# Choice of experts on 128 candidate cells with 16-bit matches, roots taken from sums of squares, and weightings between the two remainders of a slab in V

## The chip, the cores and the metric

The kernel runs on one core of a Trainium2 chip. The metric is the device time of one execution in microseconds (us), lower is better; of several runs the median is taken. The engines are TensorE (PE in the profile's rows), VectorE (DVE), ScalarE (ACT), GpSimd (POOL) and the queues that issue DMAs (SP for SyncE's). Each runs its own list of instructions in order and waits on semaphores for the others.

## The reference

Two small transformer stacks, one behind the other, on 256 tokens of width 1024. The first has gated linear attention, then sliding-window attention, each followed by a PEER layer; the second has an mLSTM mixer, an MLA mixer and two MLPs. Everything is in float32. What the change touches is the choice in PEER, and the norms:

```python
def rmsnorm(x, g):
    y = x * lax.rsqrt(jnp.mean(x * x, axis=-1, keepdims=True) + EPS)

def block(xb):                                   # 128 tokens
    q = (xb @ w_q).reshape(128, 8, 256)          # 8 heads
    s1 = jnp.einsum('phd,nd->phn', q[..., :128], subkeys[0])
    s2 = jnp.einsum('phd,nd->phn', q[..., 128:], subkeys[1])
    v1, i1 = lax.top_k(s1, 16)                   # of 128 keys
    v2, i2 = lax.top_k(s2, 16)
    cand = (v1[..., :, None] + v2[..., None, :]).reshape(128, 8, 256)
    cs, ci = lax.top_k(cand, 16)
    e = i1[ci // 16] * 128 + i2[ci % 16]         # expert of 16384
    g = jax.nn.softmax(cs, axis=-1)
    a = gelu(einsum('pd,phkd->phk', xb, u_tab[e]))
    return einsum('phk,phkd->pd', g * a, v_tab[e])
```

## The kernel before

Weights stream from HBM in slabs of 128 x 2048 numbers through a ring of two slabs; SyncE issues a half slab as soon as the remainder of the half that it replaces is made. Each half slab is a **tile** of 128 x 1024. To multiply in float32 accuracy the tile is split: ScalarE rounds it into split_hi (L1580), and the remainder split_lo = tile - split_hi is made by VectorE (L1627, in split_lo_vector) or by GpSimd (L1590). TensorE then multiplies split_hi with both parts of the activations and split_lo with the high part.

PEER does not gather rows. The **U stage** multiplies all 16384 rows of u_tab (slabs 0 to 63, tiles 0 to 127) with the tokens and applies gelu; the **V stage** multiplies the results, weighted by the routes (0 for experts that weren't chosen), with all of v_tab. The choice of experts runs on VectorE during U. It is done in 4 batches of 2 heads for the first 128 tokens (i = 0), whose weights GpSimd scatters into a table in HBM with 128 indirect DMAs per layer (L1603), and 4 batches for the other 128 tokens (i = 1), whose routes are made later from one-hot products ("route groups" of 8 tokens).

A batch (choose_batch_vector) has four searches of the 16 best of 128 scores (top16: MAX8, FIND_INDEX8, MATCH_REPLACE8, MAX8, FIND_INDEX8), then for each head the sum of 16 x 16 values (L1894) and a search on these 256 cells. Then, in two halves (part), the cell number is shifted or masked (L1906), cast (L1908), compared with 0 to 15 for all 32 choices (L1911, 512 elements), multiplied by the ids (L1918), and summed (L1923). L1928 and L1931 put the two ids together.

What stands where on VectorE is set by a small planner in the code, UTiles: every piece of the choice calls paced.after(us) with an estimate, and one split_lo is put in for every 1.55 estimated us. GpSimd makes the remainders of the first POOL_SLABS = 6 slabs (tiles 0 to 11), so the planner puts none in until HEAD_START = 33.0 estimated us are spent; the first then waits until GpSimd's twelve are made. ScalarE takes the exponentials of the weights of batch b at slab EXP_AT[b].

In V a slab of VectorE is: the routes of the next slab merged (L1972), in every even slab below 32 a route group (L1809, L1811 compare, L1815 twice weights), then for each of two tiles the remainder of the gate (L1625) and of the tile (L1627).

A norm is a chain over two engines: ScalarE's squares with their sum, VectorE's mean plus EPS (the "var" step: L581, L540, L3066, or L922 and, where a row's sum comes in two parts, L927), ScalarE's root (L525, L535, L894, L3060), VectorE's reciprocal (L933, L545), VectorE's scaling.

## Time and profile before

| | us |
|---|---|
| median of 3 runs | 2544.81 (2544.06 to 2552.29) |
| the profiled execution | 2548.69, span 2547.1 |
| TensorE busy | 2453.3 (96%) |
| VectorE busy | 2059.7 (81%) |
| ScalarE busy | 1241.6 (49%) |
| GpSimd busy | 660.8 (26%) |

The span is the time from the profile's first instruction to its last, and all times in rows count from its start. A row of the timeline joins neighbouring instructions of the same kind (x16) and gives in brackets how long the engine stood idle before it and who ended that. Layer 0's U stage is at 223 to 612 us, its V stage up to about 980; layer 1's are at 1146 to 1536 and up to about 1900. The engines work side by side, so a busy share says little: what counts is who was waited for where TensorE stood still.

### The profile page before, as it was taken

The page shows a single profiled execution, that of the slowest core. Times are in us where ns is not written, and L with a number is a line of the kernel's source. Part 1 is how long each engine was busy: PE and PEld are TensorE (multiplying, and loading weights), DVE is VectorE, ACT ScalarE, POOL GpSimd, SP SyncE. Part 2 cuts the span into 40 slices and gives each one's busy share as a digit, 9 for nine tenths or more (in the row PEclk, how much of TensorE's full clock was granted, in tenths as well). Part 3 has the DMA queues.
Part 4 walks back from the last instruction along what each step waited for, and adds up shares of the span by engine and source line. Part 5 has one row for each costly group of instructions (what it writes and reads, how often), then busy time and mean ns, then how long its engine had stood idle before and what let it go on. Part 6 is the DMA issues. An engine that isn't in the chain of part 4 may idle for free.

```text
span 2547.1 us, 42626 instructions
## 1 busy us (share of the span) xinstructions
PE 2453.3 (96%) x15130; PEld 2139.6 (84%) x15130; DVE 2059.7 (81%) x3721; ACT 1241.6 (49%) x1793; POOL 660.8 (26%) x547
## 2 busy tenths in 40 slices
PE   6999899999999999998999999999999999998998
PEld 4779899888888877898998888888878799877987
DVE  7889999788778889869998788778887888777754
ACT  5544544655444545445545555444445454335443
POOL 2114576772000001016778740000111000110000
PEclk8999999999999999999999999999999999999999
DMA  9976787776667887364777766669987557963554
GB/s 360 342 264 222 218 216 187 189 172 214 208 207 251 305 294 271 124 226 141 181 182 191 181 176 226 205 205 305 309 281 259 204 204 269 319 238 137 174 182 149
DMA packets 226190, 572.37 MB, mean 225 GB/s; under 512 B 55777, under 2 KB 86753, under 8 KB 225778
## 3 DMA queue, kind: packets, MB, share of 16 engines
q1 hardware_dynamic: 122674, 431.56, 50.2%
q0 software_dynamic: 70000, 120.43, 17.3%
q10 hardware_dynamic: 33360, 18.36, 2.4%
q8 instruction: 90, 1.47, 0.2%
q14 instruction: 66, 0.54, 0.1%
HBM read 550.20 MB, written 20.06 MB: 224 GB/s over the span
## 4 chain that ended last, share of the span: by engine, by line
PE 80%; DVE 11%; DMA 4%; ACT 2%; issue 2%; SPq 0%; POOL 0%; DVEq 0%; ACTq 0%; POOLq 0%
PE ps L2091 26%; PE ps L1547 9%; PE ps L1528 8%; PE ps L2835 7%; PE ps L761 5%; PE ps L1551 5%; PE ps L2817 5%; PE ps L1480 5%; PE ps L1532 4%; PE ps L2821 2%; DMA ring<-in_stream 2%; PE ps L1835 1%; ACT split_hi L1580 1%; DVE split_lo L1627 1%; DVE gate L941 1%
## 5 line engine op out<-in xcount | busy, mean ns | idle before, releaser
L1580 ACT ACTIVATE split_hi<-ring 128x1024 fp32r<-128x1024 f32 x760 | 800.7, 1056 | 725.1 <-PE ps L1532 197.4
L1627 DVE TENSOR_TENSOR split_lo<-ring,split_hi 128x1024 fp32r<-128x1024 f32 x676 | 822.7, 1220 | 194.2 <-ACT split_hi L1580 188.3
L1603 POOL DMA_INDIRECT routes<-small x256 | 465.3, 1818 | 176.4 <-issue 90.8
L1577 ACT ACTIVATE gate_hi<-gate 128x256 fp32r<-128x256 f32 x252 | 105.6, 419 | 367.6 <-PE ps L2091 356.0
L2091 PE MATMUL ps<-split_hi,gate_hi 128*128 128x512 f32 x1024 | 280.9, 394 | 2.5 <-DVE gate_lo L1625 1.7
L2091 PE MATMUL ps<-split_hi,gate_lo 128*128 128x512 f32 x1024 | 277.1, 390 | 2.7 <-DVE gate_lo L1625 2.6
L2091 PE MATMUL ps<-split_lo,gate_hi 128*128 128x512 f32 x1024 | 277.9, 391 | 0.0
L1528 PE MATMUL ps<-h_parts,split_hi 128*128 128x256 f32 x2048 | 269.3, 285 | 0.0
L1547 PE MATMUL ps<-h_parts,split_hi 128*128 128x512 f32 x1024 | 259.3, 395 | 0.2
L1528 PEld LDWEIGHTS ps<-h_parts,split_hi 128*128 128x128 f32 x2048 | 257.5, 194 | 0.0
L2091 PEld LDWEIGHTS ps<-split_hi,gate_lo 128*128 128x128 f32 x1024 | 191.4, 188 | 46.2 <-DVE gate_lo L1625 5.7
L2091 PEld LDWEIGHTS ps<-split_lo,gate_hi 128*128 128x128 f32 x1024 | 190.9, 188 | 45.0 <-DVE split_lo L1627 5.4
L2091 PEld LDWEIGHTS ps<-split_hi,gate_hi 128*128 128x128 f32 x1024 | 189.3, 188 | 43.4 <-ACT split_hi L1580 3.9
L1625 DVE TENSOR_TENSOR gate_lo<-gate,gate_hi 128x256 fp32r<-128x256 f32 x252 | 106.5, 422 | 131.5 <-ACT split_hi L1580 131.5
L1547 PEld LDWEIGHTS ps<-h_parts,split_hi 128*128 128x128 f32 x1024 | 183.8, 189 | 33.3 <-issue 0.5
L408 POOL DMA_DIRECT2D mod_w<-in_mod x64 | 34.0, 532 | 657.9 <-DVE strip_part L369 657.9
L449 POOL DMA_DIRECT2D small<-in_mod x104 | 55.3, 532 | 489.2 <-DVE modc L369 461.2
L1532 PE MATMUL ps<-h_parts,split_lo 128*128 128x256 f32 x1024 | 146.3, 286 | 17.5 <-DVE split_lo L1627 17.5
L1532 PEld LDWEIGHTS ps<-h_parts,split_lo 128*128 128x128 f32 x1024 | 134.0, 195 | 18.2 <-DVE split_lo L1627 17.9
L1551 PEld LDWEIGHTS ps<-h_parts,split_lo 128*128 128x128 f32 x1024 | 139.7, 190 | 10.2
L1551 PE MATMUL ps<-h_parts,split_lo 128*128 128x256 f32 x1024 | 142.6, 282 | 0.0
L369 DVE CUSTOM_DVE_ANT_0 small<-small,gate,cols 128x1024 f32<-128x1024 f32 x104 | 131.9, 1279 | 5.7 <-DMA small<-in_mod 5.7
(413 smaller groups left out, 3736.3 us busy)
## 6 DMA issues: line engine op xcount, KB each, us to landing
ring<-in_stream SPq DMA_DIRECT2D x776, 512.0 KB, 4.8
small<-in_mod POOLq DMA_DIRECT2D x104, 512.0 KB, 5.9
mod_w<-in_mod POOLq DMA_DIRECT2D x64, 512.0 KB, 5.6
gate<-in_mod POOLq DMA_DIRECT2D x44, 512.0 KB, 7.1
routes<-u_part SPq DMA_DIRECT2D x16, 1024.0 KB, 8.4
small<-routes ACTq DMA_DIRECT2D x120, 128.0 KB, 5.4
gate<-in_mod SPq DMA_DIRECT2D x8, 512.0 KB, 16.2
routes<-small POOLq DMA_INDIRECT x256
```

Source lines behind the costliest of these rows:

```text
L369: return nc.vector.tensor_tensor_reduce(out=w, in0=w, in1=c_act, scale=1.0, scalar=start, op0=ALU.mult, op1=ALU.add, accum_out=out)
L761: return nc.tensor.matmul(ps[:, banks[2 * nb + i], :], src[:, b * per + n, i * P:(i + 1) * P], w[:, b % 2, at_:at_ + BANK], start=(b == n ...
L1480: ins = nc.tensor.matmul(out, w[:, b % 2, c * P:(c + 1) * P], src[:, c, :], start=(c == 0 and w is split_hi and src is hi), stop=(c == DC ...
L1528: nc.tensor.matmul(out, split_hi[:, e, c * P:(c + 1) * P], part[:, c, :], start=(part is hT_hi and c == 0), stop=False)
L1532: ins = nc.tensor.matmul(out, split_lo[:, e, c * P:(c + 1) * P], hT_hi[:, c, :], start=False, stop=(c == DC - 1))
L1547: nc.tensor.matmul(ps[:, bank, :].rearrange("p (a n) -> p a n", a=2), split_hi[:, e, c * P:(c + 1) * P], h_parts[:, :, c, :], start=(c == ...
L1551: ins = nc.tensor.matmul(ps[:, bank, SEQ:2 * SEQ], split_lo[:, e, c * P:(c + 1) * P], hT_hi[:, c, :], start=False, stop=(c == DC - 1), ski ...
L1580: nc.scalar.activation(split_hi[:, e, :], ring[:, slot, e * D:(e + 1) * D], ACT.Copy).then_inc(hi_made, 1)
L1603: g.eng.indirect_dma_start(out=routes, out_offset=bass.IndirectOffsetOnAxis(ap=r_index[:, b, n:n + 1].bitcast(U32), axis=0), in_=r_weight[ ...
L1627: nc.vector.tensor_tensor(split_lo[:, e, :], ring[:, (START[name] + j) % RING, e * D:(e + 1) * D], split_hi[:, e, :].bitcast(F32), ALU.sub ...
L2091: return nc.tensor.matmul(ps[:, 2 * nb + n, :], g[:, e, n * P:(n + 1) * P], w[:, e, nb * BANK:(nb + 1) * BANK], start=opens, stop=True, sk ...
L2835: return nc.tensor.matmul(ps[:, 4 + 2 * nb + n, :], h[:, c0, n * P:(n + 1) * P], w[:, e, nb * BANK:(nb + 1) * BANK], start=(first and h is ...
```

## The change

**Choice.** The sum is made for both heads at once and on 128 cells: ranks 0 to 7 of the first side with all 16 of the second; the last eight of these cells, which can't be among the 16 best, are written over with ranks 8 to 15 of the first side plus the best of the second. The search on cells so covers 128 instead of 256. Each half of the matching has one more small step (c_rank, which undoes the overwriting, written twice per choice in 16 bits), and match, product and ids are 16-bit. rank_half, the numbers 0 to 15 in 16 bits, is cast once per layer. The planner's estimates follow, HEAD_START goes from 33 to 23, EXP_AT from 5, 7, 12, 18 to 5, 8, 14, 20.

**Norms.** The var step goes: the root is taken with scale 1/n and a bias, either EPS or, where the sum has two parts, the first part's mean plus EPS (L922 stays for that, now tile_part_vector).

**V.** A route group is cut in two: the two comparisons stay ahead of the slab's remainders, the two weightings stand between the first and the second.

```diff
-POOL_SLABS, HEAD_START = 6, 33.0
-EXP_AT = [5, 7, 12, 18, 42]
+POOL_SLABS, HEAD_START = 6, 23.0
+EXP_AT = [5, 8, 14, 20, 42]
...
+        def root_scalar(a, out, squares, n, mark, rest=None):
+
+            a.wait_ge(scalar_steps, a.n)
+            nc.scalar.activation(out, squares, ACT.Sqrt, scale=1.0 / n, bias=eps[:, 0:1] if rest is None else rest) \
+                .then_inc(scalar_steps, a.step(mark))
...
-        def tile_var_vector(v, name, s, i, whole):
+        def tile_part_vector(v, name, s, i):
 
             v.wait_ge(*when(f"{name}.ss{i}0"))
-            nc.vector.tensor_scalar(stat_col(s, "var" if whole else "part", i), stat_col(s, "ss", i), 1.0 / D, EPS,
-                                    ALU.mult, ALU.add).then_inc(vector_steps, v.step(f"{name}.var{i}"))
-            if not whole:
-                v.wait_ge(*when(f"{name}.ss{i}1"))
-                v.wait_ge(vector_steps, v.n)
-                nc.vector.scalar_tensor_tensor(out=stat_col(s, "var", i), in0=stat_col(s, "ss", i, 1), scalar=1.0 / D,
-                                               in1=stat_col(s, "part", i), op0=ALU.mult, op1=ALU.add) \
-                    .then_inc(vector_steps, v.step(f"{name}.var{i}"))
+            nc.vector.tensor_scalar(stat_col(s, "part", i), stat_col(s, "ss", i), 1.0 / D, EPS, ALU.mult, ALU.add) \
+                .then_inc(vector_steps, v.step(f"{name}.part{i}"))
...
+            nc.vector.tensor_tensor(
+                cand.rearrange("p h (a b) -> p h a b", b=TOPK),
+                sides[:, :, 0, 0:half].unsqueeze(3).to_broadcast([P, PER, half, TOPK]),
+                sides[:, :, 1, :].unsqueeze(2).to_broadcast([P, PER, half, TOPK]), ALU.add) \
+                .then_inc(vector_steps, v.step())
+            v.wait_ge(vector_steps, v.n)
+            nc.vector.tensor_tensor(cand[:, :, CELLS - half:], sides[:, :, 0, half:],
+                                    sides[:, :, 1, 0:1].to_broadcast([P, PER, half]), ALU.add) \
+                .then_inc(vector_steps, v.step())
+            paced.after(0.8)
             for hh in range(PER):
                 n = hh * TOPK
                 v.wait_ge(vector_steps, v.n)
-                nc.vector.tensor_tensor(
-                    cand.rearrange("p (a b) -> p a b", a=TOPK),
-                    top_v[:, 2 * hh, :].unsqueeze(2).to_broadcast([P, TOPK, TOPK]),
-                    top_v[:, 2 * hh + 1, :].unsqueeze(1).to_broadcast([P, TOPK, TOPK]), ALU.add) \
-                    .then_inc(vector_steps, v.step())
-                v.wait_ge(vector_steps, v.n)
-                top16(v, cand, cand2, w[:, n:n + TOPK], c_i[:, n:n + TOPK])
-                paced.after(2.83)
+                top16(v, cand[:, hh, :], cand2, w[:, n:n + TOPK], c_i[:, n:n + TOPK])
+                paced.after(1.57)
...
-                ranks = match.rearrange("p a b c -> p (a b) c")
+                nc.vector.scalar_tensor_tensor(
+                    out=c_rank, in0=c_cell.unsqueeze(2).to_broadcast([P, ROWS_B, PAIR]), scalar=scalar,
+                    in1=c_pf.unsqueeze(2).to_broadcast([P, ROWS_B, PAIR]), op0=op0, op1=op1) \
+                    .then_inc(vector_steps, v.step())
+                v.wait_ge(vector_steps, v.n)
                 nc.vector.tensor_tensor(
-                    ranks, c_pf.unsqueeze(2).to_broadcast([P, ROWS_B, TOPK]),
-                    iota[:, 0:TOPK].unsqueeze(1).to_broadcast([P, ROWS_B, TOPK]), ALU.is_equal) \
+                    match.rearrange("p c (k q) -> p c k q", q=PAIR),
+                    c_rank.unsqueeze(2).to_broadcast([P, ROWS_B, TOPK // PAIR, PAIR]),
+                    rank_half.rearrange("p (k q) -> p k q", q=PAIR).unsqueeze(1)
+                    .to_broadcast([P, ROWS_B, TOPK // PAIR, PAIR]), ALU.is_equal) \
                     .then_inc(vector_steps, v.step())
-                paced.after(0.9)
+                paced.after(1.0)
...
-                if slab < 32 and slab % 2 == 0:
-                    routes_group_vector(v, groups + slab // 2)
+                grouped = slab < 32 and slab % 2 == 0
+                if grouped:
+                    group_equal_vector(v, groups + slab // 2)
                 for e in range(2):
                     split_lo_vector(v, f"v{l}", slab // 8, slab % 8, e)
+                    if grouped and e == 0:
+                        group_weigh_vector(v, groups + slab // 2)
```

VectorE in layer 0's U stage, at its first split_lo (tile 12; L1627 before, L1604 after). Before, the end of batch 1:

```order
L1923 TENSOR_REDUCE small<-small 128x32
L1906 TENSOR_SCALAR small<-small 128x32
L1908 CAST small<-small 128x32
L1911 TENSOR_TENSOR small<-small,iota 128x512
L1918 TENSOR_TENSOR small<-small 128x512
L1923 TENSOR_REDUCE small<-small 128x32
L1627 TENSOR_TENSOR split_lo<-ring,split_hi 128x1024
L1951 TENSOR_REDUCE stat<-small 128x2
```

The same place after (L1876 casts the ids, L1879 and L1885 are the sums):

```order
L1876 CAST small<-small 128x64
L1879 TENSOR_TENSOR small<-small 128x256
L1885 TENSOR_TENSOR small<-small 128x2x8
L1696 MAX small<-small 128x8
L1698 MAX_INDEX small<-small 128x8
L1699 MATCH_REPLACE small<-small 128x128
L1701 MAX small<-small 128x8
L1703 MAX_INDEX small<-small 128x8
L1604 TENSOR_TENSOR split_lo<-ring,split_hi 128x1024
L1954 TENSOR_REDUCE stat<-small 128x2
```

The first split_lo has moved from behind batch 1's last reduction to behind its first search on cells; what is left of batch 1 follows it.

VectorE behind the first MLP's predecessor, where a mixer's output is normed and added and the next norm begins (at 2036 us of the trace before). Before:

```order
L941 TENSOR_TENSOR gate<-ps,gate 128x512 x2
L922 TENSOR_SCALAR stat<-stat 128x1
L927 SCALAR_TENSOR_TENSOR stat<-stat 128x1
L933 RECIPROCAL stat<-stat 128x1
L954 SCALAR_TENSOR_TENSOR x<-gate,stat,x 128x512 x2
L922 TENSOR_SCALAR stat<-stat 128x1
L927 SCALAR_TENSOR_TENSOR stat<-stat 128x1
L941 TENSOR_TENSOR gate<-ps,gate 128x512 x2
```

After:

```order
L919 TENSOR_TENSOR gate<-ps,gate 128x512 x2
L906 TENSOR_SCALAR stat<-stat 128x1
L911 RECIPROCAL stat<-stat 128x1
L932 SCALAR_TENSOR_TENSOR x<-gate,stat,x 128x512 x2
L906 TENSOR_SCALAR stat<-stat 128x1
L919 TENSOR_TENSOR gate<-ps,gate 128x512 x2
```

L927 is gone in both places; the rest stands in the same order.

VectorE in V, an even slab with a route group. Before:

```order
L1809 TENSOR_TENSOR small<-small 128x512
L1811 TENSOR_TENSOR small<-small 128x1024
L1815 TENSOR_TENSOR small<-small 128x512 x2
L1625 TENSOR_TENSOR gate_lo<-gate,gate_hi 128x256
L1627 TENSOR_TENSOR split_lo<-ring,split_hi 128x1024
L1625 TENSOR_TENSOR gate_lo<-gate,gate_hi 128x256
L1627 TENSOR_TENSOR split_lo<-ring,split_hi 128x1024
```

After:

```order
L1786 TENSOR_TENSOR small<-small 128x512
L1788 TENSOR_TENSOR small<-small 128x1024
L1602 TENSOR_TENSOR gate_lo<-gate,gate_hi 128x256
L1604 TENSOR_TENSOR split_lo<-ring,split_hi 128x1024
L1797 TENSOR_TENSOR small<-small 128x512 x2
L1602 TENSOR_TENSOR gate_lo<-gate,gate_hi 128x256
L1604 TENSOR_TENSOR split_lo<-ring,split_hi 128x1024
```

The two weightings (L1815, now L1797) have moved behind the first tile's two remainders.

## Rows read from the trace of the kernel before

**Rows 1.** The page, part 4: shares of the chain that ended last.
```profile
PE 80%; DVE 11%; DMA 4%; ACT 2%; issue 2%; SPq 0%; POOL 0%; DVEq 0%; ACTq 0%; POOLq 0%
```
**Rows 2.** Who waited for whom, TensorE: us in total, times, longest.
```profile
PE ps L1532 <- DVE split_lo L1627: 17.5, 2, 8.8
...
PE ps L639 <- DVE gate L550: 2.6, 3, 1.1
```
**Rows 3.** Timeline of TensorE, layer 0, U: start us, us, what [idle before].
```profile
256.37 1.12 PE L1532 MATMUL ps<-h_parts,split_lo 128*128 128x256 f32 x8
...
259.25 1.12 PE L1532 MATMUL ps<-h_parts,split_lo 128*128 128x256 f32 x8
...
271.05 2.07 PE L1532 MATMUL ps<-h_parts,split_lo 128*128 128x256 f32 x8 [8.76 <-DVE split_lo L1627]
...
275.81 1.12 PE L1532 MATMUL ps<-h_parts,split_lo 128*128 128x256 f32 x8
```
**Rows 4.** Timeline of TensorE, layer 1, U.
```profile
1182.17 1.12 PE L1532 MATMUL ps<-h_parts,split_lo 128*128 128x256 f32 x8
...
1193.97 2.08 PE L1532 MATMUL ps<-h_parts,split_lo 128*128 128x256 f32 x8 [8.77 <-DVE split_lo L1627]
...
1202.53 1.12 PE L1532 MATMUL ps<-h_parts,split_lo 128*128 128x256 f32 x8
```
**Rows 5.** Stretches: length, busy us of PE, PEld, DVE, ACT, POOL, granted clock, DMA.
```profile
264.00:265.00 1.00, 0.00 (x0) 0.00 (x0) 0.86 (x5) 0.00 (x0) 0.00 (x0) 0.94 0.10 37
265.00:266.00 1.00, 0.00 (x0) 0.00 (x0) 0.93 (x3) 0.00 (x0) 0.00 (x0) 0.50 0.00 0
```
**Rows 6.** Timeline of VectorE, layer 0: batches 0 and 1 of the choice.
```profile
222.24 0.29 DVE L1719 MAX8 small<-gate 128x8 f32<-128x128 f32 x1
...
235.04 2.32 DVE L1906 TENSOR_SCALAR small<-small 128x32 uint32<-128x32 uint32 x1
...
241.15 0.69 DVE L1923 TENSOR_REDUCE small<-small 128x32 f32<-128x512 f32 x1
...
251.96 0.29 DVE L1719 MAX8 small<-gate 128x8 f32<-128x128 f32 x1
...
258.36 0.20 DVE L1890 CAST small<-small 128x64 f32<-128x64 uint32 x1
258.59 0.43 DVE L1894 TENSOR_TENSOR small<-small 128x256 f32<-128x256 f32 x1
...
261.43 0.43 DVE L1894 TENSOR_TENSOR small<-small 128x256 f32<-128x256 f32 x1
...
264.69 0.18 DVE L1906 TENSOR_SCALAR small<-small 128x32 uint32<-128x32 uint32 x1
...
269.78 1.22 DVE L1627 TENSOR_TENSOR split_lo<-ring,split_hi 128x1024 fp32r<-128x1024 f32 x1
```
**Rows 7.** Timeline of GpSimd, layer 0: one of its remainders, and the last.
```profile
234.90 2.41 POOL L1590 TENSOR_TENSOR split_lo<-ring,split_hi 128x1024 fp32r<-128x1024 f32 x1 [0.43 <-ACT split_hi L1580]
...
255.06 2.41 POOL L1590 TENSOR_TENSOR split_lo<-ring,split_hi 128x1024 fp32r<-128x1024 f32 x1 [0.46 <-ACT split_hi L1580]
```
**Rows 8.** Groups of VectorE by form, 216 to 620 us: busy us, mean ns.
```profile
L1815 DVE TENSOR_TENSOR small<-small 128x512 f16<-128x512 f16 x34 | 12.8, 418 | 0.0
```
**Rows 9.** VectorE's L927: its group, then the timeline at a transition.
```profile
L927 DVE SCALAR_TENSOR_TENSOR stat<-stat 128x1 f32<-128x1 f32 x16 | 2.6, 160 | 1.9 <-ACT gate L889 0.5
...
2043.31 0.15 DVE L922 TENSOR_SCALAR stat<-stat 128x1 f32<-128x1 f32 x1
2043.56 0.16 DVE L927 SCALAR_TENSOR_TENSOR stat<-stat 128x1 f32<-128x1 f32 x1
```
**Rows 10.** Timelines in V, a slab with a group: VectorE's remainder, TensorE's use.
```profile
702.26 1.22 DVE L1627 TENSOR_TENSOR split_lo<-ring,split_hi 128x1024 fp32r<-128x1024 f32 x1
...
704.17 1.07 PE L2091 MATMUL ps<-split_lo,gate_hi 128*128 128x512 f32 x4
```
**Rows 11.** Who waited for whom, 216 to 620 us.
```profile
DVE split_lo L1627 <- ACT split_hi L1580: 34.1, 36, 1.6
```

134 lines of the change are left out of this document (60 added, 74 removed).

## The prediction

> **What bounds the kernel now.** I read the chain that ended last first: TensorE is 80% of it, VectorE 11% [rows 1]. So what VectorE does is worth time only where TensorE stands still for it. The list of who waited for whom gives these places [rows 2]: one wait of 8.8 us in each PEER layer, both in the U stage, 17.5 us in all, and small waits behind the norms, such as 2.6 us behind the gated heads.
>
> In the U stage of layer 0, TensorE takes a tile in 2.88 us: the products with split_lo start at 256.37 and 259.25 [rows 3]. The next were due at 262.13 and start at 271.05, 8.92 us late. They belong to tile 12, the first whose split_lo VectorE makes (GpSimd makes tiles 0 to 11). The granted clock has then fallen from 2.4 to 1.2 GHz: it is 0.94 of full speed in the slice 264 to 265 us and 0.50 in the next [rows 5]. From 271.05 to the next tile's 275.81 are 4.76 us instead of 2.88, so the low clock costs another 1.88. In layer 1 the start is due at 1182.17 + 2.88 = 1185.05 and comes at 1193.97, again 8.92 late, and the two tiles up to 1202.53 take 8.56 us instead of 5.76, 2.80 more [rows 4]. **The two stops cost 17.84 + 4.68 = 22.5 us.**
>
> VectorE is late because it runs the choice of two whole batches first: from 222.24 to 269.78 without a pause [rows 6]. Batch 0 takes 29.7 us of that (to 251.96), batch 1 17.8 us. Both hold the same instructions. The difference is in batch 0's small steps: the shift of L1906 takes 2.32 us at 235.04 and 0.18 us at 264.69. Six instructions of batch 0 are stretched like this one, by 11.4 us together. GpSimd is then making split_lo (2.41 us each, one every 2.88 us, the last starting at 255.06 [rows 7]), and a stretched instruction ends as GpSimd's does. The searches (MAX8 and its kin) and the reduction are not held: the one at 241.15 takes 0.69 us inside such a span.
>
> **The choice and HEAD_START.** Costs, each from a row: four searches on 128 scores take 258.36 - 251.96 = 6.40, so 1.60 each. A head on 256 cells takes 261.43 - 258.59 = 2.84, with its sum. Batch 1 in the new order is 6.40, the cast, the sum over both heads and the small second sum (0.23 + 0.46 + 0.21, small steps like the 0.18 at 264.69 plus 0.03 between), and, after one search on 128 cells (1.60), the first split_lo, since HEAD_START is now 23. That is 8.9 us from the start of batch 1 against 17.8.
>
> Batch 0 needs more care. Its own work shrinks by some 2 us (two heads at 1.60 + 1.60 + 0.67 instead of 5.68; each half of the matches has one step more, while match and product drop to 0.42, the price of a 16-bit product of 512 elements [rows 8]). But each half now has five exposed steps instead of four. I laid the new order over GpSimd's grid with the rule of the rows: an exposed step that starts inside GpSimd's 2.4 us goes on 0.14 us before its end, and the steps that follow pass as long as they start before GpSimd's next start. The same rule put over the old order ends batch 0 at 252.3, where the trace has 252.05. The new order is held seven times (second sum, copy of the best, both shifts, both matches, the last combination) instead of six. Batch 0 therefore still ends at 252.1, in the same gap of GpSimd. The first split_lo then starts at 261.0 and ends at 262.1, just when TensorE wants it. In layer 1 the same sum gives 1185.04 against 1185.05. So both stops go, and the clock has no reason to fall: **22.5 us**.
>
> This is tight in one way only. The product passes in the gap because it starts 0.45 us after the match resumed, some 0.15 us before GpSimd's next start. Each gap missed costs one round of GpSimd, 2.88 us, per layer. If the match ran at 0.69 us, as 32-bit passes over 512 elements do (the reduction above), two gaps are missed; if only the product did, one. I take 0.42 because L1815 has the same form (16-bit, innermost pairs); bounds 0.42 and 0.69.
>
> The Trainium skill (GPSIMD Engine Reference, Key points) says that GpSimd shares its SBUF interfaces with VectorE and contends with instructions in a two-port mode or with two SBUF inputs. By that rule the 16-bit matches are as exposed as the 32-bit ones, and halving them frees nothing. The held and free steps above agree. Were every exposed step held, as the rule taken alone has it, the time would be that of the second rival below.
>
> After tile 12 VectorE has no lead left, so I laid its steps against the grid of 2.88 us up to tile 64, with ScalarE's pieces and the moved exps of EXP_AT. The work between two splits averages 1.5 us beside the 1.22 us of a split; the margin starts at 1.1 us and is smallest, 0.15 us, at tile 22. The same count for the old order comes down to nothing at its worst, and there the trace shows no wait. Cost 0, bounds 0 and 3 us. The index chain for GpSimd's scatter starts earlier with the first weights, by as much as V does.
>
> **The norms.** The second half of the variance step (L927) goes, 16 times at 160 ns [rows 9]; the whole ones and the head ones too (four of L540 on VectorE). At the end of the transition at 2043 us the first half of the step (L922) ends at 2043.46 and L927 at 2043.72. Without L927 the root starts behind the first half, so it and the reciprocal come 0.26 us sooner. Where the root is waited for less closely the gain is 0.16 to 0.20. I take 14 of 16 on the path (two stand before the x_kept DMA) at 0.24 = 3.4, 0.4 for the whole ones, and 1.2 for the head norms, where TensorE waits 2.6 us for gated heads [rows 2] and where the order of VectorE no longer delays ScalarE's second squares. **5.0 us**, bounds 2.5 (0.16 each, nothing from the heads) and 6.5. ScalarE now waits for its own squares; no row has that hop, I take it as the 0.03 us between dependent steps, bounds 0 and 0.1 each (3 us in all). The table loads stay in number.
>
> **V.** VectorE finishes the first remainder of a slab with a group at 702.26 + 1.22 = 703.48, and TensorE starts on it at 704.17 [rows 10]. With the two weightings (0.75 us) behind it, it has 1.4 us of room instead of 0.7, but nobody was waiting. The second remainder waits for ScalarE in both orders. TensorE's products of the group come after this slab. Gain 0; if the cover were gone, 0.75 us in each of 30 groups.
>
> **Sum.** 22.5 + 5.0 = 27.5 us off the profiled execution's 2548.7 (span 2547.1) is 2521.2. The median of the runs lies 3.9 us under it, so 2544.8 - 27.5 = **2517.3**.
>
> **Rivals.**
> A missed gap: one product falls behind GpSimd's next start in one or both layers. For it: a margin of 0.15 us. Against: the rule reproduces the old order to 0.3 us. It gives back 2.9 to 5.8 us, and if the clock falls too (in layer 0 it fell 2.7 us after TensorE stopped), up to 4.7 more: 2520 to 2528.
> Every exposed step is held: if the exposure decides alone, batch 0 ends only with GpSimd's last tile, at 257.5, and the first split_lo ends at 257.5 + 0.2 + 8.9 + 1.2 = 267.8 (much as with matches at 0.69), 5.7 us late instead of 8.9. Then 3.2 us per layer are won and the clock still falls: 2544.8 - 6.4 - 5.0 = 2533.
> The choice doesn't come earlier in time at all (some other step fills the place): the norms alone, 2540.
> Slower: VectorE becomes the bound of U. GpSimd issues 128 scatters per layer, and if these held the 64 16-bit steps of both layers as its products hold the others, at up to 2.32 us more, that is 148 us, less VectorE's idle time in U (34.1 us in layer 0 [rows 11], as much put down for layer 1): 2544.8 + 148 - 68 - 27.5, about 2597. It decides from (68 + 27.5) / 64 = 1.5 us a step. Against: L1815 has 418 ns beside those very scatters.
>
> **How the numbers follow.** Forecast 0.62, missed gap 0.18, all held 0.08, norms alone 0.08, slower 0.04. The low end is the norms at their upper bound (1.5 us) and the spread of a median (the three runs span 8 us, so some 4): 2512. The high end is the missed gaps (2528) with the norms at their lower bound: 2530. It leaves out the last three cases, 0.20 together. A change under 0.3% (7.6 us) can't be told from none. Faster: 0.62 + 0.18 + 0.08 = 0.88; same 0.08; slower 0.04.
>
> **What would show it.** In the profile after: no TensorE wait for split_lo of 8.8 us in either layer, and a granted clock of 1.00 around 265 and 1190; batch 0 of the choice ending within 0.3 us of 252.1; the match and product at 0.42 us outside GpSimd's spans; roots 0.03 us behind their squares or parts; slabs of V with groups at the old pace. It would be wrong if a wait of 3 or 6 us stayed at tile 12 (a gap missed), or if new waits for split_lo stood at tiles 13 to 60.

## The result and the profile after

| | before | after |
|---|---|---|
| median of 6 runs, us | 2546.23 (2541.48 to 2552.29) | 2525.22 (2521.93 to 2532.64) |
| ratio, 95% interval | | 0.9918 (0.9902 to 0.9934) |
| the profiled execution, us | 2548.7 | 2523.89 |
| its span, us | 2547.1 | 2522.3 |

The change takes off 21 us, 17 to 25 by the interval; in the profiled pair the spans differ by 24.8. Forecast were 27.5 us off, 2517.3, with a range of 2512 to 2530. The sign and the mechanism of the two stops came out, 6 us of the size didn't.

In the page of the kernel after, the chain that ended last is TensorE's by 86% where it was 80% [rows 1], and VectorE's by 7% instead of 11%. The waits of TensorE (who waited for whom: us in total, times, longest) begin with these two:

```profile
PE ps L605 <- DVE gate L568: 16.7, 1, 16.7
PE ps L1130 <- ACT hT L585: 6.2, 4, 2.0
```

The line that stood at the head of it, split_lo with 17.5 us in 2 waits [rows 2], is gone, and in the whole list none of the U stage's matmuls (L1505, L1509, L1524, L1528) waits for a split_lo. The timeline of TensorE shows the place, layer 0 and then layer 1 (start us, us, what):

```profile
258.95 1.12 PE L1509 MATMUL ps<-h_parts,split_lo 128*128 128x256 f32 x8
261.85 1.22 PE L1509 MATMUL ps<-h_parts,split_lo 128*128 128x256 f32 x8
264.83 1.12 PE L1509 MATMUL ps<-h_parts,split_lo 128*128 128x256 f32 x8
...
1182.53 1.12 PE L1509 MATMUL ps<-h_parts,split_lo 128*128 128x256 f32 x8
1185.41 1.12 PE L1509 MATMUL ps<-h_parts,split_lo 128*128 128x256 f32 x8
```

Tile 12 was due at 258.95 + 2.88 = 261.83 and starts at 261.85; before it started 8.92 late [rows 3, 4]. The granted clock stays at its upper level of 2.4 GHz where it fell to 1.2 [rows 5], and is 1.00 from 1189 to 1191 us in layer 1 too; of each stretch the last three numbers are clock, DMA share and GB/s:

```profile
264.00:265.00 1.00, 1.00 (x11) 1.00 (x10) 0.93 (x7) 0.00 (x0) 1.00 (x1) 1.00 0.84 225
265.00:266.00 1.00, 1.00 (x10) 1.00 (x10) 1.00 (x2) 0.79 (x1) 0.70 (x2) 1.00 0.99 373
```

And the timeline of VectorE in layer 0, from the last small steps of batch 0 to the first remainder (three of the seven held steps are left out), with three of GpSimd's remainders under it:

```profile
234.73 2.31 DVE L1942 COPY stat<-small 128x2 f32<-128x2 f32 x1
...
237.51 2.41 DVE L1902 TENSOR_SCALAR small<-small 128x32 uint32<-128x32 uint32 x1
...
240.44 2.62 DVE L1911 TENSOR_TENSOR small<-small 128x512 f16<-128x512 f16 x1
243.09 0.42 DVE L1921 TENSOR_TENSOR small<-small 128x512 f16<-128x512 f16 x1
...
250.07 1.57 DVE L1931 SCALAR_TENSOR_TENSOR small<-small 128x32 f32<-128x32 f32 x1
251.68 0.24 DVE L1934 TENSOR_SCALAR small<-small,token 128x32 int32<-128x32 f32 x1
251.83 0.29 DVE L1696 MAX8 small<-gate 128x8 f32<-128x128 f32 x1
...
258.79 0.17 DVE L1885 TENSOR_TENSOR small<-small 128x16 f32<-128x16 f32 x1
...
260.59 1.21 DVE L1604 TENSOR_TENSOR split_lo<-ring,split_hi 128x1024 fp32r<-128x1024 f32 x1
```

```profile
240.37 2.40 POOL L1567 TENSOR_TENSOR split_lo<-ring,split_hi 128x1024 fp32r<-128x1024 f32 x1 [0.48 <-ACT split_hi L1557]
243.25 2.53 POOL L1567 TENSOR_TENSOR split_lo<-ring,split_hi 128x1024 fp32r<-128x1024 f32 x1 [0.48 <-ACT split_hi L1557]
...
249.01 2.58 POOL L1567 TENSOR_TENSOR split_lo<-ring,split_hi 128x1024 fp32r<-128x1024 f32 x1 [0.44 <-ACT split_hi L1557]
```

The match of L1911 is 16-bit work of 0.42 us (that is what it takes at 267.61, beside no remainder of GpSimd's) and takes 2.62: it starts 0.07 us behind GpSimd's instruction of 240.37 and ends 0.29 us behind that one's end at 242.77. The product of L1921 starts at 243.09, 0.16 us before GpSimd's next one, and takes 0.42. Held seven times, batch 0 gives way to batch 1 at 251.83 (251.96 before [rows 6]), and the first remainder ends at 261.80, 0.05 us before the matmul that uses it starts.

Where the 24.8 us of the two spans lie, from the start of the same matmul in both traces: 10.7 at tile 12 of layer 0 and 11.6 at tile 12 of layer 1 (22.3 together), 0.8 in the rest of the two U stages, 2.2 between the last matmul of the second V and the first MLP's loop, 1.1 between the two MLPs and 0.4 behind the second. The two MLPs give 1.7 and 0.7 back. All the rest, the way to the first U, the stretch between the layers and both V stages, adds up to the last 0.4; these parts differ by up to 6 us from one profile to another.

### The profile page after: what moved, and what is told of

Same layout as the page of the kernel before. It is cut to its first block, busy times and chain, and to the rows that moved or that the text cites. A ratio compares the mean times of both kernels' runs of the same rounds, so it can differ in the third digit from the quotient of the medians.

```text
span 2522.3 us, 42648 instructions
## 1 busy us (share of the span) xinstructions
PE 2448.7 (97%) x15130; PEld 2134.3 (85%) x15130; DVE 2026.9 (80%) x3740; ACT 1246.1 (49%) x1793; POOL 656.4 (26%) x548
## 4 chain that ended last, share of the span: by engine, by line
PE 86%; DVE 7%; DMA 3%; ACT 2%; issue 2%; SPq 0%; POOL 0%; DVEq 0%; ACTq 0%; POOLq 0%
PE ps L2097 26%; PE ps L1505 10%; PE ps L1524 9%; PE ps L2838 7%; PE ps L742 6%; PE ps L1457 5%; PE ps L1509 5%; PE ps L1528 5%; PE ps L2820 5%; PE ps L2824 2%; PE ps L1821 1%; DMA ring<-in_stream 1%; ACT split_hi L1557 1%; DVE gate L919 1%; DMA gate<-in_mod 1%
## 5 line engine op out<-in xcount | busy, mean ns | idle before, releaser
L1604 DVE TENSOR_TENSOR split_lo<-ring,split_hi 128x1024 fp32r<-128x1024 f32 x676 | 823.8, 1219 | 197.6 <-ACT split_hi L1557 193.5
L1554 ACT ACTIVATE gate_hi<-gate 128x256 fp32r<-128x256 f32 x252 | 105.2, 418 | 369.3 <-PE ps L2097 357.8
L1505 PE MATMUL ps<-h_parts,split_hi 128*128 128x256 f32 x2048 | 266.8, 283 | 0.0
L1524 PE MATMUL ps<-h_parts,split_hi 128*128 128x512 f32 x1024 | 258.9, 395 | 0.2
L1505 PEld LDWEIGHTS ps<-h_parts,split_hi 128*128 128x128 f32 x2048 | 254.9, 192 | 0.0
L1524 PEld LDWEIGHTS ps<-h_parts,split_hi 128*128 128x128 f32 x1024 | 183.8, 189 | 33.1 <-issue 0.5
L1528 PEld LDWEIGHTS ps<-h_parts,split_lo 128*128 128x128 f32 x1024 | 139.7, 190 | 10.0
L1509 PE MATMUL ps<-h_parts,split_lo 128*128 128x256 f32 x1024 | 143.9, 283 | 0.0
L1528 PE MATMUL ps<-h_parts,split_lo 128*128 128x256 f32 x1024 | 142.6, 282 | 0.0
L1509 PEld LDWEIGHTS ps<-h_parts,split_lo 128*128 128x128 f32 x1024 | 132.1, 192 | 0.1
```

The lines of the kernel that those rows point to most:

```text
L1505: nc.tensor.matmul(out, split_hi[:, e, c * P:(c + 1) * P], part[:, c, :], start=(part is hT_hi and c == 0), stop=False)
L1509: ins = nc.tensor.matmul(out, split_lo[:, e, c * P:(c + 1) * P], hT_hi[:, c, :], start=False, stop=(c == DC - 1))
L1524: nc.tensor.matmul(ps[:, bank, :].rearrange("p (a n) -> p a n", a=2), split_hi[:, e, c * P:(c + 1) * P], h_parts[:, :, c, :], start=(c == ...
L1528: ins = nc.tensor.matmul(ps[:, bank, SEQ:2 * SEQ], split_lo[:, e, c * P:(c + 1) * P], hT_hi[:, c, :], start=False, stop=(c == DC - 1), ski ...
L1604: nc.vector.tensor_tensor(split_lo[:, e, :], ring[:, (START[name] + j) % RING, e * D:(e + 1) * D], split_hi[:, e, :].bitcast(F32), ALU.sub ...
```

## Experiments

The kernels are told in the order of the questions. Each time stands beside runs of the kernel before on the same chip; ratios are to those. The ratio is estimated from all the runs and is not the quotient of the two medians; it can differ from that by up to 0.0015 (3.7 us). Where "the starts of the matmuls" are named, the same matmul was looked up in two traces and the times between two such starts compared.

| kernel | median, us | before, us | ratio (95%) |
|---|---|---|---|
| choice | 2524.02 | 2546.38 | 0.9906 (0.9888 to 0.9923) |
| head23 | 2527.68 | 2546.38 | 0.9912 (0.9893 to 0.9930) |
| norms | 2548.39 | 2546.38 | 1.0007 (0.9993 to 1.0021) |
| v_order | 2546.01 | 2546.38 | 0.9988 (0.9976 to 1.0000) |
| gap_step | 2540.63 | 2547.40 | 0.9975 (0.9964 to 0.9985) |
| head29 | 2548.47 | 2547.40 | 1.0003 (0.9992 to 1.0013) |
| after_again | 2528.20 | 2547.40 | 0.9930 (0.9913 to 0.9947) |
| norm_five | 2559.20 | 2547.40 | 1.0052 (1.0038 to 1.0066) |
| root_forms | 2525.91 | 2548.38 | 0.9909 (0.9892 to 0.9925) |
| choice_again | 2523.10 | 2548.38 | 0.9903 (0.9886 to 0.9920) |
| eps_in_stat | 2522.08 | 2547.36 | 0.9897 (0.9879 to 0.9915) |
| eps_tile_alone | 2529.12 | 2547.36 | 0.9928 (0.9911 to 0.9946) |

### One part at a time

**choice**: the kernel before with the new choice, HEAD_START 23 and the new EXP_AT; norms and V stay as they were.

> The kernel before with the new choice, HEAD_START 23 and the moved exps, without norms and V order. My theory: 22.5 us less than before (both waits of 8.8 us and the low clock behind them gone), batch 0 of the choice ending at 252, the first split_lo at about 262. Rival (the changes overlap, so that the parts sum to more than the whole): 24 us or more.

22.4 us less by the medians; the starts of the same matmuls give 22.7 us in the two U stages. That is the whole change within the intervals, and under the 24 us of the rival.

**v_order**: the kernel before with the weightings of a route group moved.

```diff
-                if slab < 32 and slab % 2 == 0:
-                    routes_group_vector(v, groups + slab // 2)
+                grouped = slab < 32 and slab % 2 == 0
+                if grouped:
+                    group_equal_vector(v, groups + slab // 2)
...
+                    if grouped and e == 0:
+                        group_weigh_vector(v, groups + slab // 2)
```

> The kernel before with the weightings of a route group between the two remainders of a slab in V, nothing else. My theory: 0 us, since TensorE waits for neither; slabs of V with a group keep 11.49 us a pair. Rival: the wobble of 1 us seen in V's second half comes from it, then the first half of V would be unchanged and slabs 32 to 63 slower.

The median moves by 0.4 us. Through the slabs with groups, the distance between the two traces stays at 2.95 us in layer 0 and 3.94 in layer 1, so the order in V gives nothing. The rival's sign is there in this one trace (V's second half is 2.3 us slower in layer 0 and 0.9 in layer 1), but not over all of them: layer 0's V takes 367.1 us in the mean of the seven profiles with the new order (366.1 to 368.4) and 366.9 in the seven without (365.0 to 369.3), layer 1's 366.8 and 366.7.

**norms**: the kernel before with root_scalar and tile_part_vector as in the change.

> The kernel before with the change of the norms alone (no second step on VectorE, the root with scale and bias). My prediction gave it 5.0 us: then the median lies near -5 and the waits for split_lo of 8.8 us stay. Rival, from the trace after: TensorE's start of layer 0's U stage came only 0.3 us sooner, and the gain reappears only from the second layer on, so the norms are worth 2 to 4 us. A third: ScalarE's wait for its own squares costs what the step saved, 0 us.

1.8 us faster to 5.3 us slower by the interval: the 5.0 us of the forecast aren't there. What lies between is worked out below, from the traces. Both stops of 8.8 us stay in its profile.

**head23**: the old choice, only begun less far ahead of the first remainder; EXP_AT and TURN_AT follow.

```diff
-POOL_SLABS, HEAD_START = 6, 33.0
-EXP_AT = [5, 7, 12, 18, 42]
-TURN_AT, ROUTES_FROM = 44, 48
+POOL_SLABS, HEAD_START = 6, 23.0
+EXP_AT = [5, 9, 15, 21, 45]
+TURN_AT, ROUTES_FROM = 46, 48
```

> The kernel before with HEAD_START 23 alone, the old choice kept (exps at slabs 5, 9, 15, 21, 45 and the turn at 46, so that the planner's order still fits). The question is whether the cheaper choice is needed at all. Theory A (only when the first split_lo stands counts): it then starts after batch 1's four searches, at 251.96 + 6.40 = 258.4, and both stops and the low clock go as with the new choice; the heavier pieces between the splits that follow (3.0 us beside 1.2) cost 0.2 to 1.1 us in three places per layer, so 22.5 - 3.4, about 19 us less than before. Theory B (the cheaper choice is what makes room): VectorE falls behind from tile 13 on, and waits for split_lo add up to 10 us or more per layer, at most a few us won.

Both stops are gone with the old choice as well. The timeline of TensorE at tile 12, layer 0, has its usual 2.88 us:

```profile
258.50 1.12 PE L1532 MATMUL ps<-h_parts,split_lo 128*128 128x256 f32 x8
261.38 1.12 PE L1532 MATMUL ps<-h_parts,split_lo 128*128 128x256 f32 x8
264.26 1.12 PE L1532 MATMUL ps<-h_parts,split_lo 128*128 128x256 f32 x8
```

By the starts of the matmuls it wins 22.6 us at the two stops and loses 0.9 of it in the rest of U, 21.7 in all; the new choice alone has 22.7 and the whole change 23.1. By the medians it is 18.7 us faster (about 19 expected). Theory B, that VectorE falls behind and TensorE waits 10 us or more per layer, is out. What the cheaper choice adds to the earlier place is about 1 us in the traces, less than the times can tell apart.

### Does the place decide, or the amount of work?

**head29**: the kernel after, with the new, cheaper choice, and the first remainder later.

```diff
-POOL_SLABS, HEAD_START = 6, 23.0
+POOL_SLABS, HEAD_START = 6, 29.5
```

> The kernel after with HEAD_START 29.5 for 23.0 and nothing else: VectorE makes the first split_lo only behind the whole of batch 1 of the choice. Theory (the place of the first split_lo decides, not how much the choice costs): batch 1 without split_lo in it ends some 5.7 us after the place where the first split_lo ended, so tile 12 is 5.5 to 6 us late in each layer and the clock falls; 12 to 16 us over the kernel after, 2536 to 2540. Rival (the cheaper searches give the gain, the place only moves it): TensorE's stop would be 1 us or less, 2524 to 2527.

20.3 us slower than after_again beside it: the whole gain is lost again with the cheaper choice still in. TensorE stops at tile 12:

```profile
268.69 2.07 PE L1509 MATMUL ps<-h_parts,split_lo 128*128 128x256 f32 x8 [6.87 <-DVE split_lo L1604]
```

Tile 12 is 7.0 us late in both layers, where 5.5 to 6 were expected (the row's 6.87 is the idle time alone). With the low clock behind it, it costs 9.3 us in layer 0 and 9.0 in layer 1 against the kernel after. That is 4 us less than the two stops of the kernel before, so the cheaper choice is worth that much where the first remainder stands behind it. Another cost was not expected at all: at the start of V, VectorE waits for the first routes, and TensorE stands still until VectorE has used them. That TensorE waits for VectorE is read from the times; its row names no releaser (timeline of VectorE, then of TensorE):

```profile
609.94 0.43 DVE L1975 TENSOR_TENSOR gate<-gate,small 128x256 f32<-128x256 f32 x1 [5.37 <-DMA small<-routes]
```

```profile
611.41 0.81 PE L2097 MATMUL ps<-split_hi,gate_hi 128*128 128x512 f32 x2 [4.16 <-issue]
```

The choice feeds GpSimd's scatters: the last one starts at 598.29 here and at 570.76 in the kernel after. Against the kernel after, the start of V loses 5.2 and 4.6 us in the two layers. Choosing later costs at both ends of U.

### The gaps between GpSimd's instructions

**gap_step**: the kernel after with one small copy between match and product, in both halves of batch 0.

```diff
+                if i == 0 and b == 0:
+                    v.wait_ge(vector_steps, v.n)
+                    nc.vector.tensor_copy(c_pf, c_cell).then_inc(vector_steps, v.step())
```

> The kernel after, with one small copy more between the match and the product of both halves of batch 0 of the choice (i = 0), in each PEER layer; the copy's result isn't used. It is worth some 0.2 us of work. Theory (gaps of GpSimd): the copy starts in the gap between two of GpSimd's split_lo, the product after it no longer does and is held for one of GpSimd's instructions more, in both halves; batch 0 ends two of GpSimd's rounds later (252 becomes 257.5) and the first split_lo of VectorE ends near 267.7 in layer 0 and 1190.6 in layer 1, so TensorE stops for 5.6 us at tile 12 in each layer and its clock falls to 1.2 GHz behind it for 1.9 to 2.8 us of loss. Time: 11 to 16 us over the kernel after, 2536 to 2541. Rival (only the sum of the work counts): 0.8 us of copies in 4 places, at most 1 us of TensorE's time; 2524 to 2527.

Four copies of 0.18 us in the whole kernel make it 12.4 us slower than after_again. The timelines of VectorE and of GpSimd say how:

```profile
240.23 2.61 DVE L1911 TENSOR_TENSOR small<-small 128x512 f16<-128x512 f16 x1
242.88 0.18 DVE L1919 COPY small<-small 128x32 f32<-128x32 f32 x1
243.09 2.64 DVE L1924 TENSOR_TENSOR small<-small 128x512 f16<-128x512 f16 x1
...
251.74 2.63 DVE L1924 TENSOR_TENSOR small<-small 128x512 f16<-128x512 f16 x1
...
257.19 0.29 DVE L1696 MAX8 small<-gate 128x8 f32<-128x128 f32 x1
```

```profile
243.04 2.40 POOL L1567 TENSOR_TENSOR split_lo<-ring,split_hi 128x1024 fp32r<-128x1024 f32 x1 [0.48 <-ACT split_hi L1557]
```

The product starts at 243.09 as it does in the kernel after; but GpSimd has started at 243.04, 0.05 us ahead of it instead of 0.16 us behind, and it takes 2.64 us instead of 0.42. Batch 1 starts at 257.19 (257.5 expected), and tile 12 starts 5.6 us late in both layers (5.6 expected; the row's 5.44 is the idle time alone):

```profile
267.22 2.08 PE L1509 MATMUL ps<-h_parts,split_lo 128*128 128x256 f32 x8 [5.44 <-DVE split_lo L1604]
```

By the starts of the matmuls the two U stages take 6.9 and 8.1 us longer than in the kernel after. The rival, that only the sum of the work counts, is out: the copies are 0.7 us of work in all. So the rival of the forecast with a missed gap was a real danger, 0.16 us away.

### Is the norms' step on the path?

**norm_five**: the kernel before with the second half of the variance step five times over.

```diff
-                v.wait_ge(vector_steps, v.n)
-                nc.vector.scalar_tensor_tensor(out=stat_col(s, "var", i), in0=stat_col(s, "ss", i, 1), scalar=1.0 / D,
-                                               in1=stat_col(s, "part", i), op0=ALU.mult, op1=ALU.add) \
-                    .then_inc(vector_steps, v.step(f"{name}.var{i}"))
+                for again in range(5):
+                    v.wait_ge(vector_steps, v.n)
+                    nc.vector.scalar_tensor_tensor(out=stat_col(s, "var", i), in0=stat_col(s, "ss", i, 1),
+                                                   scalar=1.0 / D, in1=stat_col(s, "part", i), op0=ALU.mult,
+                                                   op1=ALU.add).then_inc(vector_steps, v.step(f"{name}.var{i}"))
```

> The kernel before with the second half of the variance step (L927) done five times over instead of once, at all 16 places, each repeat waiting for the one before; the result is the same. Four repeats at 0.16 us and 0.03 us between are 0.76 us a place. If this step lies on TensorE's path at 14 places, as the forecast had it, the time grows by 10.6 us, to 2557 (and its removal must have been eaten by what the change put in its place, the dearer root). If the places are covered by other waits (a DMA, ScalarE's own chain, the slack that a slab ring gives back), it grows by less than 3 us: 2549 or less.

11.8 us slower by the medians, 10.6 by the spans. The starts of the matmuls around the places give about 0.76 us for each of 15 of the 16; only the one at 1088 us is covered. So the step does lie on TensorE's path in nearly all places, as the forecast had it. Its removal must have been paid for elsewhere.

**root_forms**: the kernel after, with one operand fewer in each of two kinds of root.

```diff
             if whole:
-                root_scalar(a, stat_col(s, "std", i), stat_col(s, "ss", i), D, f"{name}.std{i}")
+                nc.scalar.activation(stat_col(s, "std", i), stat_col(s, "ss", i), ACT.Sqrt, scale=1.0 / D) \
...
-                root_scalar(a, stat_col(s, "std", i), stat_col(s, "ss", i, 1), D, f"{name}.std{i}",
-                            rest=stat_col(s, "part", i))
+                nc.scalar.activation(stat_col(s, "std", i), stat_col(s, "ss", i, 1), ACT.Sqrt,
+                                     bias=stat_col(s, "part", i)).then_inc(scalar_steps, a.step(f"{name}.std{i}"))
```

> The kernel after with other operands in two of its roots: the 8 roots over a whole row's sum take only the factor 1/n (no bias from memory), the 16 split ones take only the bias from memory (no factor). EPS is left out in the first and the factor in the second, so the output is another. Theory (the operand from memory makes the root dearer): the first go back to about 203 ns, the second stay at 295, and the time is that of the kernel after within 1 us. Rival (the factor makes it dearer): the second fall to 203, the first stay at 295, and the time is 14 x 0.09 to 14 x 0.18 = 1.3 to 2.5 us lower.

The groups of ScalarE (us in all, mean ns), with the bias alone and with the factor alone:

```profile
L881 ACT ACTIVATE stat<-stat 128x1 f32<-128x1 f32 x16 | 4.7, 295 | 7.4 <-DVE stat L909 7.0
L876 ACT ACTIVATE stat<-stat 128x1 f32<-128x1 f32 x8 | 1.6, 203 | 0.2
```

The factor is free, the bias from memory costs 92 ns. The time doesn't part the theory (the time of the kernel after) from the rival (1.3 to 2.5 us less): the ratio of 0.9909 stands below the 0.9918 and 0.9930 of the kernel after, within the intervals. The two groups do. The Trainium skill (ScalarE: Activation LUTs, What ACT_TABLE_LOAD costs) states a price for this: each pointer operand of an activation adds about 93 ns. The trace agrees with 92.

### A pace of TensorE that the norms changed

The starts of the matmuls showed a loss where nothing was edited. In the loops of both MLPs they come every 120.0 ns in the kernels with the norms' change, and every 118.7 ns in those without, two stages excepted that are named below. The norms bring a tile of one number a partition, eps, allocated in front of the split tiles.

**after_again** and **choice_again**: the kernel after, and the choice alone, once more.

> The kernel after once more, beside the others on the same chip. If the norms and the order in V are worth nothing, as the runs of the parts say, it comes out within 2 us of the new choice alone (2524.0): ratio to the kernel before 0.990 to 0.9925. Rival (the 5 us of the norms are there but hidden in the spread of the executions): 2519 or less, ratio under 0.9895.

> The new choice with HEAD_START 23 and its EXP_AT, without the norms and the order in V, once more beside a kernel with the norms. If the norms are worth 0 to 1.5 us together (the root and what follows it cost what the step saved), the ratio to the kernel before is 0.990 to 0.993, as for the whole change. If they cost time in company with the choice, it is lower by more than 0.001 than in the whole change (0.9918 and 0.9930), 0.9905 or less.

after_again has 0.9930, above the range expected (0.990 to 0.9925); choice_again has 0.9903, under the 0.9905 named for norms that cost time. Each time the whole change stood behind the choice alone, by 0.0012 and 0.0027. Each interval is about 0.0017 wide to a side, so this alone would settle nothing.

**eps_tile_alone**: the choice alone, with the tile allocated and filled, and read by nothing.

```diff
         stat = sb("stat", [P, 64])
+        eps = sb("eps", [P, 1])
```

> The new choice without norms and V, with the tile eps allocated at the same place and filled once by GpSimd at the start; nothing reads it. Theory (the place of the tiles decides the pace): TensorE's matmuls in both MLPs every 120.0 ns instead of 118.7, and the time 3 us over the new choice alone (2523 to 2524), 2526 to 2527. Rival (the timing of the norms decides it): 118.7 ns in both MLPs, 2523 to 2524.

**eps_in_stat**: the kernel after, with eps in an unused column of stat.

```diff
-        eps = sb("eps", [P, 1])
+        eps = stat[:, 31:32]
```

> In the profiles so far TensorE's matmuls in the loops of both MLPs come every 120.0 ns in the kernels that have the norms' change, and every 118.7 ns in those that don't (one MLP of the kernel before excepted); over both MLPs that is 3.1 us. The norms bring a new tile (eps, one number a partition), allocated ahead of the split tiles, so that all tiles behind it lie elsewhere in SBUF. This kernel is the one after with eps in an unused column of stat, so that the tiles lie as before; it computes the same. Theory (the place of the tiles decides the pace): 118.7 ns in both MLPs, and some 3 us less than the kernel after: 2521 to 2523, ratio 0.989 to 0.9905. Rival (the timing of the norms in front of the MLPs decides it): still 120.0 ns, and 2524 to 2527.

The timelines of TensorE in the second MLP, where a row is 8 matmuls: the choice alone, then with the tile that nothing reads, then eps_in_stat.

```profile
2387.11 1.11 PE L2838 MATMUL ps<-mlp_hi,split_hi 128*128 128x256 f32 x8
2388.06 1.12 PE L2838 MATMUL ps<-mlp_lo,split_hi 128*128 128x256 f32 x8
```

```profile
2387.64 1.12 PE L2843 MATMUL ps<-mlp_hi,split_lo 128*128 128x256 f32 x8
2388.60 1.12 PE L2839 MATMUL ps<-mlp_hi,split_hi 128*128 128x256 f32 x8
```

```profile
2386.77 1.12 PE L2824 MATMUL ps<-mlp_hi,split_lo 128*128 128x256 f32 x8
2387.72 1.11 PE L2820 MATMUL ps<-mlp_hi,split_hi 128*128 128x256 f32 x8
```

A row comes every 0.95 us, 0.96 with the tile in place, and 0.95 again without it. 600 matmuls of a loop take 71.2 us or 72.0. All 14 MLP stages of the seven profiles with the tile have 72.0; of the 14 in the seven without it, 12 have 71.2 and two have 72.0 (the second of the kernel before, the first of eps_in_stat). So the slower pace came with the tile in every stage profiled, in eps_tile_alone without any change of the norms, and without the tile the faster one is common but not sure. The theory expected both of eps_in_stat's MLPs at 118.7, and got one.

A second stretch shows the same tile without exception, and with the other sign. The last 98 us of a U stage (between the starts of the same two matmuls, at 510.95 and 609.06 us of the trace before in layer 0) take 97.89 us in all 14 stages with the tile and 98.11 in all 14 without, eps_in_stat among these. eps_in_stat fills its column too, so it is the allocation, and with it the place of all that lies behind, that goes with the pace, and not the filling. Why a place matters so, and what sets the pace in the two exceptions, these runs don't show.

By the medians eps_tile_alone is 6 us behind choice_again, which ran on another chip (3 expected), though its profiled span of 2522.3 us isn't longer than the 2522.6 of choice; eps_in_stat at 2522.08 is as fast as anything run here. The intervals exclude neither theory. Of the kernels with this output eps_in_stat has the lowest ratio, 0.9897; against the kernel after (0.9918, 0.9930) that is likely a gain, and the slower pace, which it avoided in one of its two MLPs, is 0.8 us in every 600 matmuls.

## Why the forecast was right, and where it was not

**The two stops: right.** 22.5 us were forecast, 22.3 came, and 0.8 in the rest of U. Step by step: seven held steps in batch 0, as laid out; its last instruction's end at 251.92 for 252.1; the first remainder's end at 261.80 for 262.1, tile 12 0.02 us late; the same 0.02 us in layer 1; the clock at 2.4 GHz. The product at 0.42 us and the margin of some 0.15 us came out as 0.42 and 0.16, and gap_step showed what a miss costs. That the remainder came just in time is in part luck: the rule had reproduced the old order to 0.3 us, the forecast's own terms (252.1 + 8.9 + 1.2) add up to 262.2 against a need at 262.13, and in the trace 0.05 us were left. The rival in which GpSimd's scatters hold the 16-bit steps is out: the product at 269.09 us takes 0.42 us inside the scatter of 267.91 to 269.46.

**What the forecast gave the credit to: half right.** It summed the cheaper choice and the new HEAD_START as one edit. head23 and head29 part them: the earlier place alone, with the old choice, gives 21.7 us, and the cheaper choice with a later first remainder gives no time in the end (4 us at the stops, lost again at the starts of V).

**No new waits in U: right.** None of U's matmuls waits for a split_lo in the profile after. Of the 0.8 us won in the rest of U, 0.4 are the tile's place (97.89 us for 98.11 in each layer).

**V: right**, 0 us.

**The norms: wrong, the one term that failed.** 5.0 us were put down, some 2 came, and the lower bound of 2.5 was too high as well. Two steps failed. The first is the price of the root: the forecast took L927 away and left the root at its old length; the new root reads its bias from memory. Groups of ScalarE, the roots of the kernel after:

```profile
L517 ACT ACTIVATE stat<-stat 128x1 f32<-128x1 f32 x16 | 4.7, 295 | 7.4 <-DVE stat L906 7.0
```

The kernel before has 200 ns in the group of the same roots (there whole and split ones have one line):

```profile
L894 ACT ACTIVATE stat<-stat 128x1 f32<-128x1 f32 x24 | 4.8, 200 | 13.3 <-DVE stat L927 11.2 <-DVE stat L922 2.1
```

At the transition ahead of the first MLP, the same place as in [rows 9], the timelines of VectorE, ScalarE and VectorE of the kernel after:

```profile
2017.71 0.15 DVE L906 TENSOR_SCALAR stat<-stat 128x1 f32<-128x1 f32 x1
```

```profile
2017.89 0.30 ACT L517 ACTIVATE stat<-stat 128x1 f32<-128x1 f32 x1 [0.20 <-DVE stat L906]
```

```profile
2018.22 0.16 DVE L911 RECIPROCAL stat<-stat 128x1 f32<-128x1 f32 x1 [0.36 <-ACT stat L517]
```

The hop from the part to the root is 0.03 us, as assumed. From the part's end at 2017.86 to the reciprocal are 0.36 us. Before, it was 0.53, from 2043.46 [rows 9] to 2043.99:

```profile
2043.99 0.16 DVE L933 RECIPROCAL stat<-stat 128x1 f32<-128x1 f32 x1 [0.27 <-ACT stat L894]
```

The gain is 0.17 us, not the 0.26 of the forecast; the difference is the dearer root. At 14 places that is 2.4 us by an estimate.

The second step is ScalarE's wait for its own squares, which the forecast put at 0.03 us for the roots over a whole row, together with 0.4 us of gain for them. Timelines of ScalarE behind the first V, in the kernel before and in the kernel after:

```profile
977.71 0.19 ACT L889 ACTIVATION_READ_ACCUMULATOR gate<-x 128x1 f32 x1
977.80 0.19 ACT L894 ACTIVATE stat<-stat 128x1 f32<-128x1 f32 x1
977.89 1.04 ACT L1580 ACTIVATE split_hi<-ring 128x1024 fp32r<-128x1024 f32 x1
```

```profile
967.73 0.19 ACT L870 ACTIVATION_READ_ACCUMULATOR gate<-x 128x1 f32 x1
967.94 0.30 ACT L517 ACTIVATE stat<-stat,eps 128x1 f32<-128x1 f32 x1
968.29 1.06 ACT L1557 ACTIVATE split_hi<-ring 128x1024 fp32r<-128x1024 f32 x1
```

Before, the root started 0.10 us before the end of ScalarE's instruction ahead of it, and split_hi before the root's end. Now the root starts 0.02 us behind that end (the hop is as small as assumed, the overlap is what is lost), and split_hi comes 0.38 us later than it did. It is the wait that does this, and not the root's own length: in root_forms this root has no bias and takes 0.20 us, and split_hi is as late. The wait is also longer than it need be. The edit lets the root wait for all of ScalarE's steps so far, and the last of them is the other tile's squares; its own ended one instruction earlier. The next squares stand behind split_hi on ScalarE, and TensorE is 0.33 us later at the end of this stretch.

How much each place gives is read best between the starts of the same two matmuls, in stretches where the traces repeat to 0.2 us or better. Seven profiles have the norms' change, six don't (norm_five is left out); mean times, with the place in the trace before:

| stretch, us | with | without | difference |
|---|---|---|---|
| 123.7 to 132.2, the first head norms | 8.68 | 8.45 | +0.23 |
| 132.2 to 164.7, a norm ahead of the first U | 32.76 | 32.52 | +0.24 |
| 975.5 to 992.6, behind the first V | 17.45 | 17.11 | +0.34 |
| 1078.1 to 1092.1 | 13.80 | 13.95 | -0.15 |
| 1900.2 to 1913.1, behind the second V | 12.75 | 12.94 | -0.19 |
| 1998.1 to 2010.5, the second head norms | 12.00 | 12.45 | -0.44 |
| 2033.4 to 2045.4, three places of L927 | 11.43 | 12.04 | -0.61 |
| 2231.8 to 2292.0, behind the first MLP | 59.52 | 60.15 | -0.63 |
| 2318.7 to 2350.5, ahead of the second MLP | 31.30 | 31.81 | -0.51 |
| 2539.3 to the end | 7.35 | 7.74 | -0.39 |

But for the stretch from 1078.1 us, the seven and the six don't overlap in any of them. Together the norms are worth 2.1 us. They win 0.1 to 0.2 us for each place of L927 in the second half of the kernel, about what the estimate above says, and lose 0.8 us in the first three stretches. The head norms, put down at 1.2, win 0.44 us at one place and lose 0.23 at the other. Only the stretch at 975.5 us was followed instruction by instruction; that the other two losses have the same cause is likely and not shown.

The forecast had no term for where a tile lies. The tile that the norms bring costs 1.7 us in the first MLP where nothing disturbed its start (180.47 us for 178.77) and as much in the second of eps_tile_alone (180.72 for 178.99), 3.4 in all. In the profiled pair the second MLP of the kernel before happened to have the slow pace as well, which can be part of why the spans differ by more (24.8) than the medians (21); no run shows how often its other executions have it.

**The sum.** 22.7 (the choice and its place) + 2.1 (norms) + 0.4 (the tile in U) - 3.4 (the tile in the MLPs) is 21.8 us, against 21.0 between the medians (17 to 25). The measured 2525.2 lies in the stated range of 2512 to 2530, but not for the reason that the range was that wide: its upper part stood for missed gaps, and none was missed. What filled it is mostly the norms' 2.9 us, the tile's 3.0 net, and 1.4 us by which the kernel before itself came out above its first median.

## What to carry to other kernels

When one engine stops for another's first product, look at where that product stands in its queue before making the work ahead of it cheaper (here one number did what the cheaper choice did), and at what that work feeds further on. Where two engines hold each other up, count gaps and not microseconds: 0.05 us to the wrong side of a start cost 2.2 us. When an operation is folded into another's operands, price the operand (92 ns here for the 160 ns saved) and look at whether the instruction still overlaps with the one ahead of it (0.38 us here). Let it wait for the step that it reads and for no later one. A small new tile that moves the big ones can change a pace somewhere else, here by more than the change that brought it was worth; run it alone before crediting anything to the change.

## What the hardware did that was not expected

- A bias read from memory makes a small activation 92 ns longer (203 to 295 ns); a constant factor costs nothing.
- TensorE's pace in a loop of 128x256 matmuls has two values, 118.7 and 120.0 ns from start to start, and with a tile of one number a partition allocated ahead of the operands the slower stood in 14 of 14 stages, in two of them with nothing reading the tile; without it in 2 of 14. In U's last 98 us the same tile goes with the shorter time (97.89 for 98.11 us).
- An activation on 128x1 that waits for the one ahead of it on ScalarE loses the overlap on both its sides: it starts 0.02 us behind that one's end and no longer 0.10 ahead of it, and the next one starts 0.38 us later, with a root of 0.30 or of 0.20 us alike.
- A 16-bit product of 512 elements that starts 0.05 us behind GpSimd's instruction takes 2.64 us instead of 0.42; the searches beside the same instructions run at their usual 0.28 us.
- TensorE's clock, in gap_step, still had its upper level 4 us into the stop (1.00 in the stretch 265 to 266 us, 0.96 in the next, 0.50 behind it) and was at 1.2 GHz when it resumed; in the kernel before it was lost within 3 us of the stop [rows 5].
